# The four joints of a two-layer decoder step: last tile by thirds, two weight splits on other engines, and the last rows shared between VectorE and GpSimd

## The reference, cut to what matters

```python
def rmsnorm(x, g):
    xf = x.astype(jnp.float32)
    y = xf * lax.rsqrt(jnp.mean(xf * xf, axis=-1, keepdims=True) + EPS)
    return (y * g.astype(jnp.float32)).astype(x.dtype)
...
for l in range(DEPTH):
    m = ada_mod(c, lw['w_mod'][l], lw['b_mod'][l], N_MOD)
    h = rmsnorm(x, g[0]) * (1.0 + m[:, 1]) + m[:, 0]
    o = ...                                  # recurrent block, or attention
    x = x + m[:, 2] * rmsnorm(o, g[1])       # joint 1 (l = 0), joint 5 (l = 1)
    h = rmsnorm(x, g[2]) * (1.0 + m[:, 4]) + m[:, 3]
    o, fbuf = conv_ffn(h, ...)
    x = x + m[:, 5] * rmsnorm(o, g[3])       # joint 3 (l = 0), joint 7 (l = 1)
```

## Time and profile before

| what | us |
|---|---|
| median of 3 runs | 3171.36 |
| the profiled execution, its own time | 3171.86 |
| its span in the profile | 3170.1 |
| TensorE matmul busy | 3049.6 (96%) |
| VectorE busy | 1966.7 (62%) |
| ScalarE busy | 855.1 (27%) |
| GpSimd busy | 1190.5 (38%) |

### The profile page before, as it was taken

How to read it: one execution, slowest core, us unless ns; L and a number is a source line. 1 busy time by engine, 2 the same in 40 slices (tenths; PEclk the granted TensorE clock), 3 DMA queues, 4 the chain that set the end, 5 groups by cost and what they waited for, 6 DMA issues and landing times.

```text
span 3170.1 us, 57787 instructions
## 1 busy us (share of the span) xinstructions
PE 3049.6 (96%) x23250; PEld 2817.9 (89%) x23250; DVE 1966.7 (62%) x3517; ACT 855.1 (27%) x1339; POOL 1190.5 (38%) x801
## 2 busy tenths in 40 slices
PE   6999999999999999999979999999999999999996
PEld 4998989999999999899856666777999999999996
DVE  4677277567574856855487777402287658585676
ACT  4555131101010101302138888502131101010011
POOL 1332423444444443333216665301424444444441
PEclk8999999999999999999999999999999999999998
DMA  5222332212221212322574010275121111111112
GB/s 208 76 79 91 141 112 87 72 69 67 81 80 54 78 45 95 121 87 75 160 219 155 2 40 2 81 252 201 55 86 47 47 47 43 46 47 46 47 47 117
DMA packets 78131, 277.98 MB, mean 88 GB/s; under 512 B 8970, under 2 KB 19474, under 8 KB 74658
## 3 DMA queue, kind: packets, MB, share of 16 engines
q1 hardware_dynamic: 75298, 256.83, 24.3%
q10 hardware_dynamic: 2592, 17.73, 1.7%
HBM read 247.54 MB, written 36.27 MB: 90 GB/s over the span
## 4 chain that ended last, share of the span: by engine, by line
PE 81%; issue 5%; DVE 4%; ACT 3%; SPq 2%; POOL 1%; DMA 1%; DVEq 1%; POOLq 1%; ACTq 0%
PE PA L2128 33%; PE PB L2128 32%; PE PA L1283 2%; PE PCD L1296 2%; ACT ring L1339 1%; PE PB L1468 1%; ACT pt L1332 1%; PE PB L1307 1%; PE PA L2164 1%; PE PB L2164 1%; PE PCD L287 1%; PE PA L1307 1%; SPq L1720 1%; SPq L1721 1%; DMA mw<-in_mw 1%
## 5 line engine op out<-in xcount | busy, mean ns | idle before, releaser
L1899 POOL TENSOR_TENSOR w_hi<-w_raw,misc 128x1024 fp32r<-128x1024 f32 x192 | 382.4, 1992 | 1485.3 <-PE PA L2128 617.9
L1901 POOL TENSOR_TENSOR w_lo<-w_raw,w_hi 128x1024 fp32r<-128x1024 f32 x192 | 558.1, 2907 | 27.3
L2128 PE MATMUL PA<-hB_hi,w_hi 128*128 128x348 f32 x1272 | 273.6, 323 | 0.0
L2128 PE MATMUL PB<-hB_hi,w_hi 128*128 128x348 f32 x1272 | 272.3, 322 | 0.0
L2128 PE MATMUL PA<-hB_hi,w_lo 128*128 128x348 f32 x1272 | 271.5, 322 | 0.0
L2128 PE MATMUL PB<-hB_hi,w_lo 128*128 128x348 f32 x1272 | 271.5, 322 | 0.0
L2128 PE MATMUL PA<-hB_lo,w_hi 128*128 128x348 f32 x1272 | 271.0, 321 | 0.0
L2128 PE MATMUL PB<-hB_lo,w_hi 128*128 128x348 f32 x1272 | 271.0, 321 | 0.0
L2128 PEld LDWEIGHTS PA<-hB_hi,w_hi 128*128 128x128 f32 x1272 | 215.0, 189 | 0.4
L2128 PEld LDWEIGHTS PB<-hB_hi,w_hi 128*128 128x128 f32 x1272 | 214.9, 188 | 0.4
L2128 PEld LDWEIGHTS PB<-hB_lo,w_hi 128*128 128x128 f32 x1272 | 215.1, 188 | 0.0
(11 more groups left out here) (625 smaller groups left out, 6635.0 us busy)
## 6 DMA issues: line engine op xcount, KB each, us to landing
w_raw<-in_w SPq DMA_DIRECT2D x196, 512.0 KB, 3.7
mt<-in_mw SPq DMA_DIRECT2D x32, 1024.0 KB, 5.1
pages<-in_pages SPq DMA_DIRECT2D x64, 384.0 KB, 4.2
x_dram<-X SPq DMA_DIRECT2D x12, 1032.0 KB, 4.6
X<-x_dram SPq DMA_DIRECT2D x3, 4128.0 KB, 12.6
mw<-in_mw SPq DMA_DIRECT2D x4, 2048.0 KB, 22.6
mt_even<-in_mw SPq DMA_DIRECT2D x8, 1024.0 KB, 5.5
mt_odd<-in_mw SPq DMA_DIRECT2D x8, 1024.0 KB, 5.9
```

Source lines behind the costliest of these rows:

```text
L1899: pool.tensor_tensor(hi, raw, zero.broadcast_to([P, 1024]), ALU.add)
L1901: pool.tensor_tensor(lo, raw, hi.bitcast(F32), ALU.subtract).then_inc(sem("w_split"), 1)
L2128: mm = pe.matmul(PS[ps][:, c, 0:width], w[:, w0:w0 + P], x[:, k, c * width:(c + 1) * width], start=(k == 0 and n == 0), stop=(k == K - 1 a ...
```

## The change

- **Last tile by thirds.** The last row of squares, its addition to the sum and (joints 3 and 7) the addition of the last product to `O0` are done in three pieces of 344 tokens. The column sums wait for the thirds one after another. At joints 3 and 7 the addition of the seventh row's square goes ahead of the wait for the last tile.
- **`warm` products** ahead of the column sums: 8, 12, 8 and 8.
- **The last row's copy out of PSUM** at joints 1 and 5 goes from ScalarE to VectorE (`last_out`).
- **Splits of tiles 1 and 2** go from GpSimd to ScalarE (`first_hi`, ahead of the root) and VectorE (`first_lo`, one ahead of the reciprocal and one behind it).
- **The first row of the residual** reads the spread reciprocal from PSUM, and ScalarE's copies to `rms` come behind it. The sample columns wait for half of the transposes.
- **The root's table** is loaded by a one-element `Sqrt` ahead of the last row (joints 3, 5, 7).
- **Joint 7** gets code of its own (`last_residual`). VectorE makes output x gate x reciprocal in one instruction for each row. For rows 0, 1, 3, 4 and 6 GpSimd adds x; for rows 2, 5 and 7 ScalarE has copied x to PSUM and VectorE adds it from there. SyncE waits for each row by itself.

```diff
+    Y_POOL, Y_DVE = (0, 1, 3, 4, 6), (2, 5, 7)
+    Y_AT = {k: 26 + i for i, k in enumerate((0, 1, 3, 2, 4, 6, 5, 7))}
+    Y_X = [flat(both), flat(PA[:, 0:2, :]), flat(both)]
...
+    def square_third(act, n, i, src):
+        if i == 0:
+            act.wait_ge(sem("acc_added"), 9 * (n // 2) + 5)
+        act.activation(sq_of(n, KT - 1)[:, THIRDS[i]], src, ACT.Square).then_inc(sem("nsq_ready"), 1)
...
+    def acc_thirds(dve, n):
+        acc, sq = sq_of(n, 0), sq_of(n, KT - 1)
+        dve.drain()
+        for i in range(NCH):
+            dve.wait_ge(sem("nsq_ready"), 10 * (n // 2) + KT + i)
+            dve.tensor_tensor(acc[:, THIRDS[i]], acc[:, THIRDS[i]], sq[:, THIRDS[i]], ALU.add).then_inc(sem("acc_added"), 1)
...
+    def first_hi(act, n):
+        t, done, r = next_tiles(n)
+        act.wait_ge(sem(f"w_in{(t + 1) % 2}"), 16 * ((t + 1) // 2 + 1))
+        act.wait_ge(sem("tile_done"), done)
+        act.activation(w_hi[(t + 1) % 2], w_raw[(t + 1) % 2], ACT.Copy).then_inc(sem("first_hi"), 1)
+        act.wait_ge(sem(f"w_in{t % 2}"), 16 * ((t + 2) // 2 + 1))
+        act.activation(WX[r][0], w_raw[t % 2], ACT.Copy).then_inc(sem("first_hi"), 1)
+
+    def first_lo(dve, n, i):
+        t, done, r = next_tiles(n)
+        hi, lo = (w_hi[(t + 1) % 2], w_lo[(t + 1) % 2]) if i == 1 else WX[r]
+        dve.wait_ge(sem("first_hi"), 2 * (n // 2) + i)
+        dve.wait_ge(sem("w_split"), t + i)
+        dve.tensor_tensor(lo, w_raw[(t + i) % 2], hi.bitcast(F32), ALU.subtract).then_inc(sem("w_split"), 1)
...
     def stats(pe, n, evicted):
-        warm(pe, PC, {1: 12, 3: 26, 5: 12, 7: 16}[n])
+        warm(pe, PC, {1: 8, 3: 12, 5: 8, 7: 8}[n])
         pe.wait_ge(*evicted)
-        pe.wait_ge(sem("acc_added"), 7 * (n // 2) + 7)
         acc = sq_of(n, 0)
-        for c in range(KT + 1):
-            t = min(c * P, TOK - P)
-            mm = pe.matmul(PA[:, 0, c:c + 1], acc[:, t:t + P], ones[:, 0:1], start=True, stop=True, skip_group_check=True)
+        cols = PB[:, 2, 2 * P:2 * P + KT + 1] if n == 7 else PA[:, 0, 0:KT + 1]
+        for i, cs in enumerate(((0, 1), (2, 3, 4), (5, 6, 7, 8))):
+            pe.wait_ge(sem("acc_added"), 9 * (n // 2) + 7 + i)
+            for c in cs:
+                t = min(c * P, TOK - P)
+                mm = pe.matmul(cols[:, c:c + 1], acc[:, t:t + P], ones[:, 0:1], start=True, stop=True, skip_group_check=True)
...
@@ first_splits (GpSimd)
-            for i in range(n):
+            for i in (0, *range(3, n)):
...
@@ root (ScalarE)
             if n < 7:
+                act.wait_ge(sem("rst_ready"), n + 1)
                 for half in range(2):
-                    act.wait_ge(sem("rms_spread"), n + half)
                     act.activation(rms[:, half * 512:half * 512 + 512], PCD[half], ACT.Copy).then_inc(sem("row_out"), 1)
...
@@ residual (VectorE)
+            first_lo(dve, n, 1)
             dve.wait_ge(sem("sqrt_done"), n + 1)
             dve.reciprocal(rst, rst).then_inc(sem("rst_ready"), 1)
+            first_lo(dve, n, 2)
             dve.wait_ge(sem("x_back"), (16, 32, 48, 64)[r])
...
             def weighted(k):
-                dve.tensor_tensor(b[f"t{k % 2}_{NREG[n]}"][:, 0:NPR], src[:, k, 0:NPR], rows, ALU.mult)
+                rows = rms[:, 0:NPR] if k else flat(both)
+                return dve.tensor_tensor(b[f"t{k % 2}_{NREG[n]}"][:, 0:NPR], src[:, k, 0:NPR], rows, ALU.mult)
...
-            weighted(0)
+            dve.wait_ge(sem("rms_spread"), n + 1)
+            weighted(0).then_inc(sem("rst_ready"), 1)
             dve.drain()
             added(0)
...
+            dve.wait_ge(sem("row_out"), n + 1)
             weighted(1)
...
+        def last_out(n):
+            dve.wait_ge(sem("nsq_ready"), 10 * (n // 2) + KT + 2)
+            dve.tensor_copy(c3(O1[:, KT - 1, :]), PS[(KT - 1) % 2][:, :, 0:CH]).then_inc(sem("ev_act"), 1)
...
+            def scaled(k, to):
+                return dve.scalar_tensor_tensor(to[:, 0:NPR], O0[:, k, 0:NPR], mcol(11, k), rows, ALU.mult, ALU.mult)
+            def for_pool(i):
+                scaled(Y_POOL[i], Y_ROW[i]).then_inc(sem("x_ready"), 1)
+            def own(i):
+                k = Y_DVE[i]
+                dve.wait_ge(sem("row_out"), 6 + i + 1)
+                dve.tensor_tensor(X[:, k, 0:NPR], X[:, k, 0:NPR], Y_X[i], ALU.add).then_inc(sem("x_ready"), 1)
...
@@ GpSimd, at the end
+        for i, k in enumerate(Y_POOL):
+            pool.wait_ge(sem("x_ready"), Y_AT[k])
+            pool.tensor_tensor(X[:, k, 0:NPR], Y_ROW[i][:, 0:NPR], X[:, k, 0:NPR], ALU.add).then_inc(sem("y_pool"), 1)
...
@@ ScalarE, joint 1
+        act.wait_ge(sem("tile_done"), 24)
+        for i in range(NCH):
+            square_third(act, 1, i, PS[(KT - 1) % 2][:, i, 0:CH])
+        first_hi(act, 1)
         root(1)
```

More of the change, by code:

```diff
@@ L2072, in _ @@
         row_out(act, 8, PC)
-        for n in range(KT):
+        for n in range(KT - 1):
             act.wait_ge(sem("tile_done"), 16 + n + 1)
@@ L2082, in _, with ffn_squares @@
         ffn_act(act, 0)
-        for k in range(KT):
-            act.wait_ge(sem("sum_out"), CHUNKS * 8 - 8 + k + 1)
-            square(act, 3, k, O0[:, k, :])
+        def ffn_squares(n, l):
+            for k in range(KT - 1):
+                act.wait_ge(sem("sum_out"), 48 * l + CHUNKS * 8 - 8 + k + 1)
+                square(act, n, k, O0[:, k, :])
+            act.activation(mark, deps[0:1, :], ACT.Sqrt)
+            for i in range(NCH):
+                if i < NCH - 1:
+                    act.wait_ge(sem("sum_third"), 2 * l + i + 1)
+                else:
+                    act.wait_ge(sem("sum_out"), 48 * l + CHUNKS * 8)
+                square_third(act, n, i, O0[:, KT - 1, THIRDS[i]])
+        ffn_squares(3, 0)
+        first_hi(act, 3)
         root(3)
@@ L2098, in _ @@
             act.activation(c3(O1[:, n, :]), PS[n % 2][:, :, 0:CH], ACT.Copy).then_inc(sem("ev_act"), 1)
+        act.activation(mark, deps[0:1, :], ACT.Sqrt)
+        act.wait_ge(sem("tile_done"), 149)
+        for i in range(NCH):
+            square_third(act, 5, i, PS[(KT - 1) % 2][:, i, 0:CH])
+        first_hi(act, 5)
         root(5)
@@ L2101, in _ @@
         ffn_act(act, 1)
-        for k in range(KT):
-            act.wait_ge(sem("sum_out"), 48 + CHUNKS * 8 - 8 + k + 1)
-            square(act, 7, k, O0[:, k, :])
+        ffn_squares(7, 1)
         root(7)
+        act.wait_ge(sem("x_back"), 64)
+        for i, k in enumerate(Y_DVE):
+            act.wait_ge(*((sem("col_sums"), 4), (sem("col_sums"), 4), (sem("x_ready"), Y_AT[2]))[i])
+            act.activation(Y_X[i], X[:, k, 0:NPR], ACT.Copy).then_inc(sem("row_out"), 1)
     @block.tensor
@@ L2419, in residual @@
             b = NB[NREG[n]]
+            first_lo(dve, n, 1)
             dve.wait_ge(sem("sqrt_done"), n + 1)
             dve.reciprocal(rst, rst).then_inc(sem("rst_ready"), 1)
+            first_lo(dve, n, 2)
             dve.wait_ge(sem("x_back"), (16, 32, 48, 64)[r])
-            if n < 7:
-                dve.wait_ge(sem("rms_spread"), n + 1)
-            else:
-                dve.wait_ge(sem("rms_spread"), 7)
-            rows = rms[:, 0:NPR] if n < 7 else flat(PB[:, 0:2, :])
+            dve.wait_ge(sem("rms_spread"), n)
             normed_samples(src, PB[:, 2, P - NS:P])
@@ L2588, in _ @@
         prepare(dve, 4)
-        for k in range(6, KT):
-            acc_add(dve, 1, k)
+        acc_add(dve, 1, 6)
+        acc_thirds(dve, 1)
+        last_out(1)
         residual(0, 1, O1, 2, 4, 3)
@@ L2600, in _ @@
         smp_dve(dve)
-        for k in range(1, KT):
+        for k in range(1, KT - 1):
             acc_add(dve, 5, k)
+        acc_thirds(dve, 5)
+        last_out(5)
         residual(2, 5, O1, 8, 10, 9)
@@ L2605, in _ @@
         ffn_dve(dve, 1)
-        residual(3, 7, O0, 11)
+        last_residual()
     block.__exit__(None, None, None)
```

77 lines of the change are left out of this document (57 added, 20 removed).

## The result

The change takes 3150.70 us (median of 4 runs, 3150.09 to 3153.61); the kernel before, run beside it, 3171.59 (4 runs, 3169.67 to 3172.15). The ratio is 0.9937, 95% interval 0.9920 to 0.9954. That is 20.9 us less, where 18.1 were forecast; 3150.7 lies inside the range of 3149 to 3163. The profiled execution took 3150.87 with a span of 3149.1, against 3171.86 and 3170.1. So 21.0 us of span have to be found.

What follows compares the result with a forecast made beforehand. TensorE work is 81% of the span; the change targets TensorE's waits at four joints, one chain over four engines. Gains of 2.8 + 4.8 + 2.8 + 2.1 + 5.6 = 18.1 us give a median of 3153.3, range 3149 to 3163.

Steps and rivals of the forecast that it cites:

- Joint 1: Last product to first residual row at the first joint: 9.96 us before, 7.15 forecast, a gain of 2.8.
- joint 5: Last product to first residual row at this joint: 9.94 us before, 7.15 forecast, a gain of 2.8.
- 2.2 in all: Joints 1 and 5: the transposes (1.91 us) and the small one ahead of them take 2.2 us, to 7.05.
- Joint 3: Last product to first residual row at this joint: 12.58 us before, 7.75 forecast, a gain of 4.8.
- joint 7: Last product to first row instruction at the last joint: 9.89 us before, 7.8 forecast, a gain of 2.1.
- The tail: Eight last rows behind joint 7: 20.13 us become 13.6, less 0.95 for the last write; gain 5.6 (2.9 to 6.7).
- first kind: Last rows: VectorE's 8 instructions with factor and gate, an operand in PSUM, taken at 1.22 to 1.28 us.
- The five named terms: Gains at joints 1, 3, 5 and 7 and in the last rows: 2.8 + 4.8 + 2.8 + 2.1 + 5.6 = 18.1 us.
- Rival A: Last rows: GpSimd and VectorE exclude each other, so the rows take 25.4 us, the kernel 3165.1; chance 0.04.
- B: Splits on ScalarE and VectorE not hidden: three times 2.26 us (1.04 + 1.22) lost, 3160.1 in all; chance 0.07.
- C: Fewer `warm` products leave TensorE at 1.2 GHz in the eight rows after each joint: 25 us, 3178; chance 0.03.
- D: The chain does not shrink, another wait standing behind each one: gain under 6 us, about 3168; chance 0.04.

## Why the prediction was right

**Joint 1, forecast 2.8, measured 3.85; joint 5, 2.8 and 3.29.** The steps up to the reciprocal held: sums 1.58 after the last product (1.7 forecast), their end near 3.65 (3.85), and the reciprocal behind VectorE's subtraction, not behind the root. It started at 4.05 and 4.17, not 4.6, because I added VectorE's durations up, while instructions that follow at once overlap: three thirds of 0.51 take 1.37, and the next two start 1.14 apart at 1.23 each. The other error is the term "2.2 in all" for the transposes: at joint 1 they took 1.20, with TensorE's clock still at 1.00. All four joints before had them at 2.18, and I took those rows without asking at which clock they were made. Only about 0.5 of that 1.0 reached the first row, since VectorE was at the second subtraction and the sample columns until 0.7 behind the transposes; at joint 5 the transposes took 2.18, as forecast, and ended last.

**Joint 3, 4.8 and 4.85; joint 7, 2.1 and 2.00.** Every step of joint 3 came out within 0.1: sums to 4.90 (4.8), reciprocal at 5.24 (5.15), transposes to 7.70 (7.6). One premise was wrong and cost almost nothing: the addition that is "done early" took 3.25 beside GpSimd and delayed the thirds by 0.66, but the idle products lasted until 2.64, and the sums started at 2.76. That it cost so little is luck. My sentence that "GpSimd is silent" there is true of the splits of tiles 1 and 2, not of tile 0.

**The tail, 5.6 and 5.60.** All terms held: first kind 1.27 to 1.28, GpSimd 2.35 (2.36 taken), 13.54 on VectorE (13.6), and the last write 0.99 longer than before behind the last row (0.95).

**The total, 18.1 and 20.9.** The five named terms gave 19.6, 1.5 more than forecast, from joints 1 and 5. The rest is the 1.5 behind joint 1, which I counted as none, and terms of both signs that differ as much between executions of one program.

**The weak sentence.** "The four splits taken from GpSimd cost it nothing and save nothing there" is true of GpSimd and hid what the move is for. I used the short additions (0.52 for a third, 1.23 for a row) in every term and named the splits as what made them long, but priced the thirds as the cause of the gain and the move as a cost to be hidden. The run with the splits back shows that without the move there is no gain at joints 1 and 5 and almost none at joint 3: it is 15 to 16 us slower than the change.

**Rival A** was ruled out rightly: with one operand in PSUM VectorE takes 1.22 beside GpSimd, and the run with both in SBUF shows what it would have been, though at 1.6 us and not at the 12 less 0.95 that A had, which charged a full 2.36 five times. **B**: the reciprocal starts 0.09 and 0.21 us behind the root at joints 1 and 5, where 0.03 is the least, so the first subtraction is hidden to within 0.1 to 0.2 us; the second one is part of why VectorE comes last at joint 1. **C**: PEclk is 1.00 from 404 to 424 us and in the 20 us behind the first products of joints 3 and 5, and the mean over the span is 0.987 (0.985 before); the danger was real in another place, as the run in one piece showed, where too few idle products cost the column sums their clock. C's price was too low: 0.133 and 0.173 us are means over wide and narrow products. From one row's first product to the next row's it took 2.67 us at the upper clock (402.29 to 404.96, the change) and 4.04 where the clock stood mostly at the lower one (404.47 to 408.51, before), so a row costs about 1.4 and not 0.8. **D**: no other wait took the place.

## What to carry to other kernels

Before a short operation on VectorE's critical chain is cut into pieces, look for GpSimd instructions beside it: an operation with two SBUF operands waits for the rest of the one that is running, however narrow it is, so pieces multiply the waits; take GpSimd's work away first, or put one operand in PSUM. Idle products that bridge a wait should end just when the wait does: too many stand in the way, and with too few the clock fell in the column sums of joints 3 and 7. They are no guarantee: it also fell once with no pause to speak of. Take a duration on TensorE only together with the granted clock of its row.

## What was not expected of the hardware

Additions of 344 columns took 1.9 to 2.6 us beside GpSimd, and a multiplication of 64 columns 2.05 us, against 0.51 and 0.22 alone. The exclusion works both ways: GpSimd's additions went from 2.35 to 3.33 us. TensorE's clock fell at joint 3 within work that had no pause in the 1.1 us ahead of it. Kernels that are the same up to that point have the transposes of joint 3 at 1.20 or 2.19 us and those of joint 7 at 1.20 to 2.18 in different executions. The first row moves with them by 0.5 us at joint 3, where VectorE then comes last, and by 1.0 at joint 7. The Trainium skill, "TensorE: Matmul & The Clock Gate" (Part 1), says that the number of products at the lower clock varies from run to run of one kernel, for the products at a kernel's start. The traces agree for the middle of one: at joint 7 the nine transposes took 2.18 us in one execution of the change and 1.70 in another.
